# Building the RWKV-7 scan's triangular inverses from packed 64x64 diagonal blocks, with the level masks on VectorE

## The reference

```python
def step(state, inp):
    r_t, w_t, k_t, v_t, a_t, b_t = inp
    sa = jnp.einsum('bhij,bhj->bhi', state, a_t)
    state = (state * w_t[:, :, None, :] + sa[..., None] * b_t[:, :, None, :]
             + v_t[..., None] * k_t[:, :, None, :])
    return state, jnp.einsum('bhij,bhj->bhi', state, r_t)
...
# _peer, for each token: h heads, k experts
act = jax.nn.gelu(jnp.einsum('thkd,td->thk', u_sel, xb))
return jnp.einsum('thk,thkd->td', gate * act, v_sel)
```

## Time and profile before

| | |
|---|---|
| median of three timed runs | 4501.64 us (4489.85 to 4512.01) |
| profiled execution | 4498.14 us, span 4496.3 us |
| TensorE busy / weight loads busy | 3307.0 us (74%) / 2083.9 us (46%) |
| VectorE busy | 2523.6 us (56%) |
| ScalarE busy | 1669.0 us (37%) |
| GpSimd busy | 1269.0 us (28%) |
| mean granted clock | 0.796 |
| scans | about 160 to 285, 935 to 1135, 1997 to 2190, 3020 to 3220 us |

### The profile page before, as it was taken

The page is one execution under the profiler, slowest core; times in us unless marked ns, Lnnn a source line. Parts: engine busy times, 40 slices in busy tenths (PEclk is TensorE's granted clock), DMA queues, the critical chain, the costliest instruction groups (busy, mean ns, idle before and its releaser), DMA issues.

```text
span 4496.3 us, 60154 instructions
## 1 busy us (share of the span) xinstructions
PE 3307.0 (74%) x20472; PEld 2083.9 (46%) x20472; DVE 2523.6 (56%) x6058; ACT 1669.0 (37%) x4720; POOL 1269.0 (28%) x1140
## 2 busy tenths in 40 slices
PE   7898875678989966768879874658989984444544
PEld 5676762346556633336556652326646662111111
DVE  2322248766457357866545448776547537974554
ACT  2223124443444234343462433443353433333333
POOL 0110002245212231336322222235422212343332
PEclk8899986779989966779989985668889986555555
DMA  7212338868868878988879876878888777899997
GB/s 247 94 40 99 110 129 325 318 248 319 330 250 307 350 312 329 377 330 324 316 276 361 327 285 266 320 287 303 294 312 307 292 292 300 354 396 421 421 418 317
DMA packets 247570, 1315.37 MB, mean 293 GB/s; under 512 B 21216, under 2 KB 35168, under 8 KB 116192
## 3 DMA queue, kind: packets, MB, share of 16 engines
q0 software_dynamic: 147456, 1073.81, 61.4%
q1 hardware_dynamic: 99808, 237.72, 14.4%
HBM read 1309.34 MB, written 2.10 MB: 292 GB/s over the span
## 4 chain that ended last, share of the span: by engine, by line
PE 31%; DVE 21%; DMA 17%; PEld 9%; issue 8%; ACT 8%; DVEq 3%; ACTq 2%; PEldq 1%; POOL 0%; POOLq 0%; SPq 0%
DMA row<-uv,e_idx 12%; DVE row L1515 8%; PE bank L630 5%; PE bank L681 4%; PEld bank L667 4%; PE bank L788 3%; PE bank L667 3%; DMA weights<-w_in 2%; PE bank L999 2%; PEld bank L681 2%; PEld bank L931 2%; PE bank L779 2%; DVE reg L1414 2%; DMA weights<-w_out 1%; DMA weights<-w_ada 1%
## 5 line engine op out<-in xcount | busy, mean ns | idle before, releaser
L1896 POOL DMA_INDIRECT row<-uv,e_idx x1024 | 1116.9, 1091 | 2900.6 <-PE bank L630 2309.9
L1515 DVE CUSTOM_DVE_ANT_0 row<-row,e_rep 128x1024 f32<-128x1024 f32 x1024 | 1272.8, 1262 | 595.7 <-DMA row<-uv,e_idx 515.0
L630 PE MATMUL bank<-row,e_diag 128*32 128x256 f32 x8192 | 841.6, 498 | 827.5 <-ACT e_diag L1091 723.6
L630 PEld LDWEIGHTS bank<-row,e_diag 128*32 128x32 f32 x8192 | 197.5, 123 | 1367.8 <-ACT e_diag L1091 1012.7
L1087 ACT ACTIVATE e_ge<-e_dot 128x1 f32<-128x1 f32 x1024 | 206.8, 202 | 1567.3 <-DVE e_dot L1515 1529.0
L681 PE MATMUL bank<-hT,weights 128*128 128x256 f32 (+2 forms) x2176 | 555.7, 411 | 21.6 <-DMA weights<-w_in 13.3
L681 PEld LDWEIGHTS bank<-hT,weights 128*128 128x128 f32 (+2 forms) x2176 | 420.6, 199 | 158.2 <-issue 66.3
L667 PE MATMUL bank<-hT,weights 128*128 128x256 f32 x1536 | 357.4, 386 | 19.1 <-issue 11.6
L1091 ACT ACTIVATE e_diag<-mask,e_wg 128x32 f32<-128x32 f32 x1024 | 329.2, 321 | 73.9 <-issue 3.7
L1089 ACT ACTIVATE e_wg<-e_gate,e_ge 128x1 f32<-128x1 f32 x1024 | 301.5, 294 | 74.3 <-issue 4.3
L667 PEld LDWEIGHTS bank<-hT,weights 128*128 128x128 f32 x1536 | 285.1, 190 | 91.2 <-issue 50.1
(11 more groups left out here) (259 smaller groups left out, 3964.7 us busy)
## 6 DMA issues: line engine op xcount, KB each, us to landing
weights<-w_ada SPq DMA_DIRECT2D x48, 1024.0 KB
weights<-w_mac SPq DMA_DIRECT2D x64, 768.0 KB
weights<-w_in SPq DMA_DIRECT2D x44, 1024.0 KB
...
row<-uv,e_idx POOLq DMA_INDIRECT x1024
...
```

Of the source, the lines that this page charges most:

```text
L630: last = mm(acc_ps[g % 2][c * QT:(c + 1) * QT, 0:2 * P], e_diag[:, n % RING, :], row[n % RING][:, D + c * 2 * P:D + (c + 1) * 2 * P], star ...
L1515: V.tensor_tensor_reduce(row[r][:, 0:D], row[r][:, 0:D], e_rep[g % 2], 1.0, 0.0, ALU.mult, ALU.add, e_dot[:, r:r + 1]).then_inc(dots, 1)
L1896: pool.indirect_dma_start(row[r], None, uv, bass.IndirectOffsetOnAxis(ap=e_idx[:, j:j + 1], axis=0)).then_inc(rows_landed[r], 16)
```

## The change

In levels 0 to 5 the matrices are block-diagonal with blocks of 64, so only the two diagonal blocks of each 128x128 matrix are kept, packed: rows 0 to 63 hold the upper block, rows 64 to 127 the lower, 64 columns wide. `r_ad` holds the packed blocks of `r_ab`, `r_td` takes the place of `r_tt` in levels 1 to 5. Each 128x128 matmul becomes two of 64x64 by 64 columns, one on the array's quadrant of rows and columns 0 to 63, one on that of rows and columns 64 to 127; both write the same bank, on different partitions. `m0` is an ordinary matmul with the identity instead of a transpose. Copies and updates are 256 elements wide instead of 512. After level 5 the blocks are spread into `r_tt`; level 6 multiplies the off-diagonal block of `r_ab` directly (no mask), four matmuls of 64x64 for each of `u` and `ut`. The level masks move from GpSimd to VectorE, six instead of seven, each issued two levels ahead. GpSimd only gathers.

```diff
--- before.py
+++ after.py
-LAG = dict(POOL=-2.5, DVE=0.5, ACT=0.8, PE=2.2)
+LAG = dict(DVE=0.5, ACT=0.8, PE=2.2)
...
+        lo64, hi64 = slice(0, 64), slice(64, P)
+        blocks = (lo64, hi64)
...
-        r_tt, r_tn, r_u = (v3(at(12304 + i * 1024, 1024), 8) for i in range(3))
+        r_tt = v3(at(12304, 1024), 8)
+        r_tn, r_td, r_u = v3(at(13328, 512), 8), v3(at(13840, 512), 8), v3(ycf[:, 512:1024], 8)
         r_gs = at(14352, 1024).rearrange("p (q w h v) -> p q w h v", q=2, w=2, h=4)
-        r_m = [v3(at(15376, 1024), 8), v3(ycf, 8)]
+        r_m = [v3(at(15376, 512), 8), v3(ycf[:, 0:512], 8)]
+        r_ad = v3(at(15888, 512), 8)
+        lvl64, eye64 = lvl[:, :, 0:64], lvl[:, 6, 0:64]
...
                     elif stage == 1 and not half:
                         ps = opened("m0", t, q)
-                        need(f"level_masked{q}", 7 * t + 1)
+                        need(f"level_masked{q}", 6 * t + 1)
                         for i, x in enumerate(heads):
-                            last = nc.tensor.transpose(ps[:, i * P:(i + 1) * P], r_m[0][:, x, :], ident)
+                            for b in blocks:
+                                last = mm(ps[b, i * 64:(i + 1) * 64], r_m[0][b, x, :], ident[b, b], start=True, stop=True)
                         last.then_inc(filled("m0", t, q), 1)
                     elif 1 < stage < 8 and not half:
                         lv = stage - 1
                         ps = opened("u", t, lv, q)
-                        need(f"level_masked{q}", 7 * t + lv + 1)
+                        if lv < 6:
+                            need(f"level_masked{q}", 6 * t + lv + 1)
                         need(f"t_updated{q}", 13 * t + 2 * lv - 1)
                         for i, x in enumerate(heads):
-                            last = mm(ps[:, i * P:(i + 1) * P], r_m[lv % 2][:, x, :], r_tn[:, x, :], start=True, stop=True)
+                            if lv == 6:
+                                last = mm(ps[hi64, i * 64:(i + 1) * 64], r_ab[lo64, x, 64:P], r_tn[lo64, x, :], start=True, stop=True)
+                            else:
+                                for b in blocks:
+                                    last = mm(ps[b, i * 64:(i + 1) * 64], r_m[lv % 2][b, x, :], r_tn[b, x, :], start=True, stop=True)
                         last.then_inc(filled("u", t, lv, q), 1)
                     elif 1 < stage < 8:
                         lv = stage - 1
                         need(f"u_copied{q}", 6 * t + lv)
                         need(f"t_updated{q}", 13 * t + 2 * lv)
-                        for nm, a_, b_ in ((("tu", r_tt, r_u),) if lv < 6 else ()) + (("ut", r_u, r_tt),):
+                        for nm, a_, b_ in (("tu", r_td, r_u), ("ut", r_u, r_td)) if lv < 6 else ():
                             ps = opened(nm, t, lv, q)
                             for i, x in enumerate(heads):
-                                last = mm(ps[:, i * P:(i + 1) * P], a_[:, x, :], b_[:, x, :], start=True, stop=True)
+                                for b in blocks:
+                                    last = mm(ps[b, i * 64:(i + 1) * 64], a_[b, x, :], b_[b, x, :], start=True, stop=True)
                             last.then_inc(filled(nm, t, lv, q), 1)
+                        if lv == 6:
+                            ps = opened("ut", t, lv, q)
+                            for i, x in enumerate(heads):
+                                last = mm(ps[lo64, i * 64:(i + 1) * 64], r_u[hi64, x, :], r_tt[hi64, x, hi64], start=True, stop=True)
+                            last.then_inc(filled("ut", t, lv, q), 1)
...
-                        A(r_u[:, xs, :], ps[:, :], ACT.Copy).then_inc(freed("u", t, lv, q), 1)
+                        b = hi64 if lv == 6 else slice(0, P)
+                        A(r_u[b, xs, :], v3(ps[b, 0:256], 4), ACT.Copy).then_inc(freed("u", t, lv, q), 1)
                         act.drain().then_inc(G[f"u_copied{q}"].sem, 1)
...
+            V.tensor_copy(lvl[hi64, 0:6, 0:64], lvl[hi64, 0:6, 64:P])
+            V.tensor_tensor(eye64, ident[:, 0:64], ident[:, 64:P], ALU.add)
...
+                def level(q, lv):
+                    xs = slice(4 * q, 4 * q + 4)
+                    V.tensor_tensor(r_m[lv % 2][:, xs, :], r_ad[:, xs, :], bc(lvl64[:, lv, :].unsqueeze(1), [P, 4, 64]), ALU.mult)
+                    dve.drain().then_inc(G[f"level_masked{q}"].sem, 1)
+
                 assert lap == 0 or turns.i > max(PIECES)
+                V.memset(r_tt[hi64, :, lo64], 0.0)
                 for half_, t, q, stage in rwkv_steps():
                     xs = slice(4 * q, 4 * q + 4)
                     if stage == 0 and not half_:
                         turns.upto(plan.open_at["ab", t, 0, q])
                         if t:
                             need("y_copied", 2 * t + q - 1)
-                            need(f"level_masked{q}", 7 * t)
                         for nm, dst in (("ab", r_ab), ("kb", r_ak)):
                             for p in range(2):
                                 ps = full(nm, t, p, q)
                                 V.tensor_tensor(dst[:, 4 * q + p:4 * q + 4:2, :], v3(ps[:, :], 2), bc(tri.unsqueeze(1), [P, 2, 2 * P]), ALU.mult)\
                                     .then_inc(freed(nm, t, p, q), 1)
                                 dve.drain().then_inc(G["ab_masked"].sem, 1)
+                            if nm == "ab":
+                                for b in (lo64, hi64):
+                                    V.tensor_copy(r_ad[b, xs, :], r_ab[b, xs, b])
+                                dve.drain()
+                        level(q, 0)
+                        level(q, 1)
                     elif stage == 1 and not half_:
                         turns.upto(plan.open_at["m0", t, q])
                         if t:
                             need("sa_copied", 2 * t + q - 1)
-                        need(f"level_masked{q}", 7 * t + 1)
                         ps = full("m0", t, q)
-                        V.tensor_tensor(r_tn[:, xs, :], v3(ps[:, :], 4), bc(ident.unsqueeze(1), [P, 4, P]), ALU.add).then_inc(freed("m0", t, q), 1)
+                        V.tensor_tensor(r_tn[:, xs, :], v3(ps[:, 0:256], 4), bc(eye64.unsqueeze(1), [P, 4, 64]), ALU.add).then_inc(freed("m0", t, q), 1)
                         dve.drain().then_inc(G[f"t_updated{q}"].sem, 1)
-                        V.tensor_tensor(r_tt[:, xs, :], r_m[0][:, xs, :], bc(ident.unsqueeze(1), [P, 4, P]), ALU.add)
+                        V.tensor_tensor(r_td[:, xs, :], r_m[0][:, xs, :], bc(eye64.unsqueeze(1), [P, 4, 64]), ALU.add)
                         dve.drain().then_inc(G[f"t_updated{q}"].sem, 1)
+                        level(q, 2)
                     elif 1 < stage < 8 and half_:
                         lv = stage - 1
                         if lv < 6:
                             ps = full("tu", t, lv, q)
-                            V.tensor_tensor(r_tn[:, xs, :], v3(ps[:, :], 4), r_tn[:, xs, :], ALU.add).then_inc(freed("tu", t, lv, q), 1)
+                            V.tensor_tensor(r_tn[:, xs, :], v3(ps[:, 0:256], 4), r_tn[:, xs, :], ALU.add).then_inc(freed("tu", t, lv, q), 1)
                             dve.drain().then_inc(G[f"t_updated{q}"].sem, 1)
                         ps = full("ut", t, lv, q)
-                        V.tensor_tensor(r_tt[:, xs, :], v3(ps[:, :], 4), r_tt[:, xs, :], ALU.add).then_inc(freed("ut", t, lv, q), 1)
+                        if lv < 5:
+                            V.tensor_tensor(r_td[:, xs, :], v3(ps[:, 0:256], 4), r_td[:, xs, :], ALU.add).then_inc(freed("ut", t, lv, q), 1)
+                        elif lv == 5:
+                            V.tensor_tensor(r_tt[hi64, xs, hi64], v3(ps[hi64, 0:256], 4), r_td[hi64, xs, :], ALU.add)
+                            V.tensor_tensor(r_tt[lo64, xs, lo64], v3(ps[lo64, 0:256], 4), r_td[lo64, xs, :], ALU.add)                                .then_inc(freed("ut", t, lv, q), 1)
+                        else:
+                            V.tensor_copy(r_tt[lo64, xs, hi64], v3(ps[lo64, 0:256], 4)).then_inc(freed("ut", t, lv, q), 1)
                         dve.drain().then_inc(G[f"t_updated{q}"].sem, 1)
+                        if lv < 4:
+                            level(q, lv + 2)
...
-                    yield True
-
-            pool.wait_ge(loaded, 16 * 5)
-            for lap in range(LAPS):
-                l, h, plan = lap // 2, lap % 2, PLANS[lap]
-                turns = Turns(expert_steps(lap - 1), LAG["POOL"]) if lap else Turns()
-
-                def need(sig, k=None):
-                    pool.wait_ge(*G[sig].at(lap, k))
-
-                for half, t, q, lv in rwkv_steps():
-                    if half or lv > 6:
-                        continue
-                    xs = slice(4 * q, 4 * q + 4)
-                    turns.upto(plan.open_at[("kb", t, 1, q) if lv == 0 else ("m0", t, q) if lv == 1 else ("u", t, lv - 1, q)])
-                    if lv == 0:
-                        if t:
```

(16 more changed lines are left out.)

2 lines of the change are left out of this document (1 added, 1 removed).

## The result

The changed kernel takes 4455.29 us (median of five, 4451.23 to 4465.92) against 4494.45 for the kernel before (five runs beside it): ratio 0.9908, interval 0.9884 to 0.9933 (the ratio compares all executions of the two kernels, so it is not exactly the quotient of the medians). It is faster, by 39 us and not by 89. The profiled executions have spans of 4456.7 and 4496.3 us, mean granted clocks of 0.776 and 0.796.

A forecast was written before the change was run, and what follows sets the result against it. TensorE was taken as the fullest engine inside the scans. Savings of 20 us in lap 0 and 69 in laps 1 to 3, 89 together, gave 4498 - 89 = 4409, said as 4410 us, range 4375 to 4445 (65%).

The forecast's parts named there:

- The array time per group: TensorE in the scans: a group holds the array 0.56 us instead of 0.97, saving 27.5 us a scan at clock 1.00.
- The first rival: TensorE's two quadrants don't overlap, a group takes 1.12 us of array time; result about 4510 us; 13%.
- The chain of one level: Lap 0, from one u to the next: 2.66 us instead of 3.93, 1.27 less.
- The clock term: TensorE's granted clock falls in the scans, taking back 4 us in lap 0 and 3 in laps 1 to 3.
- The second rival: The clock eats half: TensorE granted 0.75 instead of 0.9 in all scans, result 4450 us; 10%.
- Stage 0 to 1: Start of each unit: copies and masks queue on VectorE, about 1.1 us later to the first u, once a unit.
- The rest of the sum: Scan savings: lap 0 20 us, laps 1 to 3 69 us, together 89 us.
- The forecast for line 1515: VectorE's slot line in laps 1 to 3: 1.22 us without stretched ones, as GpSimd's masks leave; 9 us a scan back.
- no change outside the scans: Everything outside the four laps' scans, including the tail after the last lap, keeps its time.
- The third rival: VectorE's masks and copies delay the slots in laps 1 to 3, 18 us a scan; result 4527 us; 5%.

The follow-up runs named there:

- masks_on_gpsimd: The changed kernel with its six narrow level masks made by GpSimd instead of VectorE: 4457.36 us, ratio 0.9900.
- masks_on_gpsimd_and_filler: masks_on_gpsimd plus 24 unread 256-column matmuls a scan where TensorE waits for ScalarE's copy of u: 4423.30 us, ratio 0.9835.
- quadrants_in_turn: The changed kernel with each group's four heads of one quadrant issued before the four of the other, not alternating: 4588.51 us, ratio 1.0195.

## Why the prediction was wrong

- **The array time per group held.** A group u of 16 records takes 0.68 us (0.74 forecast), tu and ut 1.15, and 30 to 33 us of full-clock work left each scan (27.5 forecast). The first rival is out. The Trainium skill, TensorEngine Tiling (Array Packing), "Gotcha 1: PSUM Pressure", has it that different row tiles cannot use one PSUM bank at the same time. This case's trace does not agree: both quadrants write one bank, and at the high clock the group takes 0.68, not the 1.12 that the prediction worked out for no overlap.
- **The chain of one level** held too: 2.54 us against 2.66.
- **The clock term failed, and it is the step that the prediction had wrong.** I charged 4 us in lap 0 and 3 in laps 1 to 3 together, from a bound of 16 for lap 0. The clock fell to 0.73 in lap 0, where I had worked with 1.00 going towards 0.85, and to 0.75 to 0.79 where I kept 0.87 to 0.92. In lap 0 that cost 26 us, more than the bound, and in lap 1 18. TensorE's busy time in laps 1 to 3, forecast near 143 us, was 162 to 169. What was wrong in the mechanism is that I read the clock off TensorE's busy share: with 85% busy, lap 2's scan of before was granted 0.90, and with the same 85% lap 1's scan of the changed kernel 0.76.
- **The second rival (10%)**, 4450 us at a clock of 0.75, is what happened in the sum: 4455 was measured, inside the range and outside the forecast's own. By laps it was off too: lap 0 gained nothing where it gave 10. That rival's argument against itself, that the pauses are short, was no protection: none was longer than 3.0 us in lap 0's scan. I had also the stretch with TensorE 64% busy at 0.74 before me, and took it as an end of the range.
- **Stage 0 to 1 on VectorE was counted on the wrong unit.** I charged 1.1 us to the new unit's chain. The new unit's eight VectorE instructions stand ahead of the running unit's update, which TensorE waits 2.9 to 3.0 us for, once in each two-unit stretch, where it waited 0.6 to 0.7 before. That is some 7 of the 8 us by which its idle time grew in lap 0. With the level masks on GpSimd the pause is 1.8 to 1.9. The rest of it goes by the timeline with the block copies and with tu and ut, which now end 0.9 us sooner than the product masks let VectorE go; no run takes these apart.
- **The rest of the sum came out near, but in another kernel.** With the masks on GpSimd and the clock held up by fillers, the scans took 81 us less than before (89 forecast), lap 0 by 15.9 (20 forecast), laps 1 to 3 by 22.5, 14.0 and 28.8, together 65 (69 forecast); the medians differ by 74 us (4497 to 4423), and the profiled execution, 4412.88 us, was the fastest. It shows that the slots and the transfers can let such a gain through. It does not confirm the sum: part of it is the fillers' own gain, since before with the same filler has scans only 58 us longer, and the masks are not where the change puts them. That the two numbers are close is in part luck.
- **The forecast for line 1515** (1.22 us, none stretched: the longest of line 1533 is 1.30) and for no change outside the scans held. The third rival, VectorE's masks delaying the slots, did not decide here: with the level masks on GpSimd the scans of laps 1 to 3 are no shorter (together 604.1 us against 589.8). At full width the masks cost 24 us, but half of it in lap 0's scan, where there are no slots.
- **What stays open.** Shown: in lap 0 the lower clock cost 26 us; 24 wide, useless matmuls a scan raise the clock and take 19 us from the change and 34 from masks_on_gpsimd (29 by the ratios), and 8-column ones do little. Not shown is that this is special to the change, as the kernel before gains 18 by them. With the same filler in both the change is worth 43 us (4479 to 4436), or 56 with GpSimd's masks, not much more than the 39 it shows without; but that is no comparison at equal clock, as the scans have 0.91 to 0.96 in the one and 0.81 to 0.84 in the other. No run holds the changed kernel at the clock of before without adding work, so how much of the missing 50 us is the clock's stays open outside lap 0. What it is in the packed groups that lowers the clock is not settled either: in lap 0 it falls behind the pauses of 2.9 to 3.0 us, it also falls behind those of 1.8 to 1.9 in masks_on_gpsimd, and behind the three of 1.2 to 1.3 in masks_on_gpsimd_and_filler it stays at 1.00 but for some 8 us. So the pauses are one candidate, but quadrants_in_turn has 0.62 with TensorE 91% busy. How the masks and the filler share the 32 us between 4455 and 4423 isn't separable (masks alone 2 us slower, filler alone 19 faster, both 32).
